# A one-layer mixer and mixture-of-experts step in float32: channel-major inputs for the prologue, and GpSimd in place of VectorE for the low halves of most weight units

## What is computed

```
h  = xn @ w_in                       # 1024 -> pool 512 | u 512 | v 512 | ca 512 | cg 512 | gates 3*1024
ya = pool_scale * (windowed mean of p, minus p) @ pool_w
yb = u * (tril(W_s) layer_norm(v) + b)                # chunks of 128 tokens
yc = silu(layer_norm(depthwise_conv31(ca * sigmoid(cg))))
merged = ga*(ya @ wb_pool) + gb*(yb @ wb_sgu) + gc*(yc @ wb_conv)
mixer  = merged @ w_out
moe    = top-1 of 4 groups, then top-2 of its 8 SwiGLU experts (1024 -> 512 -> 1024), 32 experts
```

## Time and profile before

| | us |
|---|---|
| median of three runs (1003.26 to 1004.27) | 1003.76 |
| the profiled execution | 1007.17 |
| its span, first to last instruction | 1005.4 |
| TensorE busy | 848.6 |
| VectorE busy | 353.4 |
| ScalarE busy | 201.4 |
| GpSimd busy | 65.8 |

### The profile page before, as it was taken

The page is one execution under the profiler, slowest core; times in us unless marked ns, Lnnn a source line. Parts: engine busy times, 40 slices in busy tenths (PEclk is TensorE's granted clock), DMA queues, the critical chain, the costliest instruction groups (busy, mean ns, idle before and its releaser), DMA issues.

```text
span 1005.4 us, 12484 instructions
## 1 busy us (share of the span) xinstructions
PE 848.6 (84%) x5203; PEld 581.2 (58%) x5203; DVE 353.4 (35%) x511; ACT 201.4 (20%) x300; POOL 65.8 (7%) x72
## 2 busy tenths in 40 slices
PE   3999999999999997997388898888878778877860
PEld 2999999999999997994133333333323232322320
DVE  3377686899577545204500000000000000000007
ACT  5321333222214323115001001100000000001003
POOL 0000000000000000000101111011101111011000
PEclk9999999999999998999599999999999999999995
DMA  9322221213315428544489999999999999999936
GB/s 296 94 85 85 84 85 54 79 49 105 106 50 181 168 63 312 196 169 163 163 323 419 419 419 419 417 418 417 421 417 419 420 419 419 419 419 419 417 151 252
DMA packets 73670, 262.16 MB, mean 261 GB/s; under 512 B 8999, under 2 KB 42947, under 8 KB 48480
## 3 DMA queue, kind: packets, MB, share of 16 engines
q1 hardware_dynamic: 68496, 252.44, 64.1%
q0 software_dynamic: 5120, 8.93, 2.4%
HBM read 256.08 MB, written 13.74 MB: 268 GB/s over the span
## 4 chain that ended last, share of the span: by engine, by line
PE 62%; DMA 19%; SPq 10%; DVE 5%; issue 2%; ACT 2%; POOLq 0%; DVEq 0%; ACTq 0%
PE ps L685 30%; DMA mem<-in_w_up_e 17%; PE ps L929 12%; SPq L550 10%; PE ps L720 9%; PE ps L950 5%; PE ps L653 1%; PE ps L917 1%; PE ps L814 1%; DMA mem<-expert_rows 1%; PE ps L940 1%; DVE xh L1669 1%; DVE xh L1676 1%; DVE mem L1635 1%; DVE xh L1668 0%
## 5 line engine op out<-in xcount | busy, mean ns | idle before, releaser
L929 PE MATMUL ps<-mem 128*64 128x512 f32 x1024 | 237.3, 618 | 28.0 <-DMA mem<-in_w_up_e 27.1
L929 PEld LDWEIGHTS ps<-mem 128*64 128x64 f32 x1024 | 81.9, 142 | 180.5 <-issue 179.3
L685 PE MATMUL ps<-x_high,w_high 128*128 128x272 f32 x640 | 173.8, 289 | 0.0
L1628 DVE TENSOR_TENSOR mem<-ps,ffn_cols 128x512 f32<-128x512 f32 x32 | 22.1, 692 | 431.1 <-PE ps L917 431.1
L685 PE MATMUL ps<-x_low,w_high 128*128 128x272 f32 x640 | 173.0, 289 | 0.0
L950 PE MATMUL ps<-mem 128*64 128x512 f32 x512 | 127.1, 642 | 14.8 <-ACT mem L1199 14.8
L685 PE MATMUL ps<-x_high,w_low 128*128 128x272 f32 x640 | 132.8, 289 | 0.0
L685 PEld LDWEIGHTS ps<-x_low,w_high 128*128 128x128 f32 x640 | 120.8, 189 | 0.1
L685 PEld LDWEIGHTS ps<-x_high,w_high 128*128 128x128 f32 x640 | 120.8, 189 | 0.1
L685 PEld LDWEIGHTS ps<-x_high,w_low 128*128 128x128 f32 x640 | 100.4, 189 | 0.0
L1266 DVE TENSOR_TENSOR w_low<-w_raw,w_high 128x2048 fp32r<-128x2048 f32 (+1 forms) x38 | 74.1, 1952 | 50.2 <-ACT w_high L1003 48.0
(11 more groups left out here) (224 smaller groups left out, 840.0 us busy)
## 6 DMA issues: line engine op xcount, KB each, us to landing
mem<-in_w_gate_e SPq DMA_DIRECT2D x32, 2048.0 KB, 34.0
mem<-in_w_up_e SPq DMA_DIRECT2D x32, 2048.0 KB, 33.8
mem<-in_w_down_e SPq DMA_DIRECT2D x32, 2048.0 KB, 34.1
w_raw<-in_w_in SPq DMA_DIRECT2D x22, 1024.0 KB, 5.1
w_raw<-in_w_out SPq DMA_DIRECT2D x4, 1024.0 KB, 6.7
mem<-expert_rows SPq DMA_DIRECT2D x4, 1024.0 KB, 9.6
xh<-in_x_prompt SPq DMA_DIRECT2D x4, 512.0 KB, 5.0
w_raw<-in_w_branch_pool SPq DMA_DIRECT2D x4, 512.0 KB, 3.5
```

The costliest lines, as they stand in the source:

```text
L685: last = pe.matmul(ps[:, 2 * r + half, 0:HT], w[:, k, c * P:(c + 1) * P], part[:, k, half * HT:(half + 1) * HT], start=(k == 0 and len(par ...
L929: last = pe.matmul(ps[g * CAP:(g + 1) * CAP, 2 + s].rearrange("p (m f) -> p m f", m=2), xgT[s][:, k % 4, (k // 4) * CAP:(k // 4 + 1) * CAP ...
L1628: v.tensor_tensor(xgT[s].rearrange("p c (h m) -> p c h m", h=2), ps[:, s].rearrange("p (c h m) -> p c h m", c=4, h=2), wide(ffn_cols[:].re ...
```

## The change

1. The host hands over x, the states, the vectors and the SGU weights with channels on partitions, and takes the new states back so. All transposes of the prologue, the two transposes of new states, the 32 tiny DMAs and 18 of the state stores go.
2. The sum of squares is taken over partitions: ACT and DVE square, DVE adds pairs, TensorE sums by a product with a column of ones, ACT takes the root, DVE inverts it and spreads it on a diagonal, TensorE broadcasts it (`ones` times `diag`) to PSUM, and DVE scales each x tile by it (`scale_x`).
3. Units 0 and 1 are split in halves of four k, and the first three column tiles are interleaved over k so that TensorE can start on tile k = 0.
4. GpSimd makes the low halves of units 2 to 37, in the order of the units, with the copies of states in its queue as well.
5. The branch for `AHEAD` in the expert loops is folded; the order of instructions stays as it was with `AHEAD = 0`.

```diff
@@ sync
-        for c in range(NCH):
-            src = d["x_prompt"][0][c * P:(c + 1) * P] if c < NCH - 1 else d["x_sample"].rearrange("b i n -> (b i) n")
-            sp.dma_start(x[0:chunk_rows(c), c], src).then_inc(x_loaded[c], 16)
-        sp.dma_start(cst[:], d["shape_constants"]).then_inc(const_loaded, 16)
...
+        sp.dma_start(cst[:, 0:CONST["before"].start], d["shape_constants"][:, 0:CONST["before"].start]).then_inc(ident_loaded, 16)
+        for i in range(KD // 2):
+            sp.dma_start(x_raw[:, 2 * i:2 * i + 2], d["x_channels"][:, 2 * i:2 * i + 2]).then_inc(x_loaded[i], 16)
+        sp.dma_start(param[:, 0:FG + KD], d["vectors"]).then_inc(param_loaded, 16)
...
+        for n in range(2):
             load_unit(n)
+        sp.dma_start(cst[:, CONST["before"].start:], d["shape_constants"][:, CONST["before"].start:]).then_inc(const_loaded, 16)
+        sp.dma_start(pool_before, d["pool_before"]).then_inc(states_loaded, 16)
+        sp.dma_start(conv_before, d["conv_before"]).then_inc(states_loaded, 16)
+        load_unit(2)
+        sp.dma_start(wsT, d["sgu_w_columns"]).then_inc(sgu_w_loaded, 16)
+        sp.dma_start(step_w, d["sgu_w_steps"]).then_inc(step_loaded, 16)
...
-                for b in range(NSEQ):
-                    r = slice(b * STEP, (b + 1) * STEP)
-                    sp.dma_start(out["pool_sample"][0][b, PH - STEP:PH], states[r, 1]).then_inc(states_stored, 16)
-                    sp.dma_start(out["conv_sample"][0][b, CH - STEP:CH], states[r, 3]).then_inc(states_stored, 16)
+                sp.wait_ge(states_out, 2)
+                sp.dma_start(out["pool_channels"], pool_after).then_inc(states_stored, 16)
+                sp.dma_start(out["conv_channels"], conv_after).then_inc(states_stored, 16)
@@ tensor
+        for i in range(KD // 2):
+            pe.wait_ge(pair_squared, i + 1)
             for c in range(NCH):
+                first = min(c * P, T - P)
+                last = pe.matmul(ps[:, 0, 0:NCH], squared_x[:, 2 * i, first:first + P], const["pick"][:, NCH - 1 - c:2 * NCH - 1 - c],
+                                 start=(i == 0 and c == 0), stop=(i == KD // 2 - 1 and c == NCH - 1))
+        pe.wait_ge(diag_ready, 1)
+        for c in range(NCH):
+            n = chunk_rows(c)
+            last = pe.matmul(ps[:, 6 + c // 4, (c % 4) * P:(c % 4) * P + n], const["ones"], diag[:, c, P - n:], start=True, stop=True)
...
+        for k in range(KD):
+            pe.wait_ge(act_took, act_has["xT", k])
+            for n, c, r in ((0, 0, 0), (0, 1, 1), (1, 0, 2)):
+                if k == 0 and c == 0:
+                    pe.wait_ge(first_low, n + 1)
+                if k == KD // 2 and c == 0:
+                    pe.wait_ge(low_ready, n + 1)
+                if r == 0:
+                    pe.wait_ge(dve_took, dve_has["xT", k])
+                last = tile_step(n, k, r, c)
...
-        state_rows(0, PH, lambda q: pext[:, q, SEQ:SEQ + PH], lambda q: pext[:, q, PH + SEQ:PH + T])
-        state_rows(4, CH, lambda q: cext[:, q, SEQ:SEQ + CH], lambda q: cext[:, q, CH + SEQ:CH + T])
@@ scalar
+        own(nc.scalar.activation(stat[:, 94:95], stat[:, 94:95], ACT.Sqrt))
+        for i in range(KD // 2):
+            act.wait_ge(x_loaded[i], 16)
+            nc.scalar.activation(squared_x[:, 2 * i], x_raw[:, 2 * i], ACT.Square).then_inc(x_squared, 1)
+        act.wait_ge(product, made["squares"])
+        nc.scalar.activation(stat[:, 5:5 + NCH], ps[:, 0, 0:NCH], ACT.Sqrt, scale=1.0 / D, bias=stat[:, 95:96]).then_inc(root, 1)
+        first_part(0, 0)
+        for k in range(4):
+            take_x(k)
+            if k < 3:
+                first_part((1, 0, 1)[k], (0, 1, 1)[k])
+        for k in range(4, KD):
+            take_x(k)
@@ vector
+        for i in range(KD // 2):
+            dve.wait_ge(x_loaded[i], 16)
+            own(v.tensor_tensor(squared_x[:, 2 * i + 1], x_raw[:, 2 * i + 1], x_raw[:, 2 * i + 1], ALU.mult))
+            dve.wait_ge(x_squared, i + 1)
+            v.tensor_tensor(squared_x[:, 2 * i], squared_x[:, 2 * i], squared_x[:, 2 * i + 1], ALU.add).then_inc(pair_squared, 1)
         dve.wait_ge(root, 1)
         own(v.reciprocal(stat[:, 10:10 + NCH], stat[:, 5:5 + NCH]))
+        v.tensor_tensor(diag, wide(ident.unsqueeze(1), [P, NCH, P]), wide(stat[:, 10:10 + NCH].unsqueeze(2), [P, NCH, P]), ALU.mult).then_inc(diag_ready, 1)
+        first_low_part(0, 0)
+        dve.wait_ge(product, made["spread"])
+        scale_x(0)
         for k in range(KD):
+            if k + 1 < KD:
+                scale_x(k + 1)
+            low_x(k)
+            if k < 3:
+                first_low_part((1, 0, 1)[k], (0, 1, 1)[k])
...
...
         glu(0)
-        low_part(3)
         glu(1)
...
         for j in range(NJ - 1):
             n = unit_no["branch", 0, j]
             merge(j, 0)
             merge(j, 1)
-            low_part(n + 2)
...
             for b in range(4):
...
-                if b in (0, 2):
-                    low_part(n + 4 + b // 2)
...
@@ gpsimd
+        pool.wait_ge(product, made["spread"])
         g.memset(pext[:, :, 0:PH], 0.0).then_inc(zeroed, 1)
+        pool.wait_ge(states_loaded, 32)
+        g.tensor_copy(pext[:, :, PH + T:]..., pool_before).then_inc(states_placed, 1)
+        g.tensor_copy(cext[:, :, CH + T:]..., conv_before).then_inc(states_placed, 1)
+        g.tensor_tensor(wsT, wsT, wide(const["causal"].unsqueeze(1), [P, KW, P]), ALU.mult).then_inc(sgu_masked, 1)
+        g.tensor_tensor(step_w, step_w, wide(const["blocks"][0:NS].unsqueeze(1), [NS, KW, NS]), ALU.mult).then_inc(steps_masked, 1)
+        def low_part(n):
+            s, kt = n % 3, depth(units[n])
+            pool.wait_ge(high_ready, n + 1)
+            g.tensor_tensor(w_low[s][:, 0:kt], w_raw[s][:, 0:kt], w_high[s][:, 0:kt].bitcast(F32), ALU.subtract).then_inc(low_ready, 1)
+        for n in range(2, 10):
+            low_part(n)
+        pool.wait_ge(p_extended, KW)
+        own(g.tensor_copy(pool_after[:, :, 0], pext[:, :, SEQ:SEQ + PH]))
...
+        for n in range(10, len(units)):
+            low_part(n)
```

More of the change, by code:

```diff
@@ L63 @@
 CONST, NCONST = _columns([
-    ("ident", P), ("causal", P), ("before", P), ("ones", P), ("blocks", NS),
+    ("ident", P), ("ones", P), ("pick", 2 * NCH - 1), ("before", P), ("causal", P), ("blocks", NS),
     ("expert", NE), ("group_of", NE), ("group", NG), ("place", P), ("block", NBLK), ("gather_row", 2 * NCH), ("scatter_row", 2 * NCH),
@@ L448, in program @@
     act_has = numbered(act_in_order)
[L450 removed]
+    dve_in_order = [("xT", k) for k in range(KD)] + tiles("ca") + tiles("pool") + ["sgu_steps"] + tiles("sgu")
     for j in range(NJ):
@@ L634, in _ @@
         sp.wait_ge(outs_stored, 16 * (1 + NCH))
-        sp.wait_ge(states_stored, 16 * (4 + 2 * NSEQ))
+        sp.wait_ge(states_stored, 16 * 2)
     @block.tensor
     def _(pe):
[L640 to L650, removed]
-            for c in range(NCH):
[L652 to L655, removed]
@@ L670, in _ @@
+        last.then_inc(product, 1)
+        pe.wait_ge(diag_ready, 1)
+        for c in range(NCH):
+            n = chunk_rows(c)
+            last = pe.matmul(ps[:, 6 + c // 4, (c % 4) * P:(c % 4) * P + n], const["ones"], diag[:, c, P - n:],
+                             start=True, stop=True)
         last.then_inc(product, 1)
@@ L691, in _, with tile_step @@
         xs = (x_high, x_low)
[L694 to L695 removed]
+        def tile_step(s, k, r, c):
             for half in range(2):
[L697 to L707 removed]
+                for w, part in ((w_high[s], x_high), (w_low[s], x_high), (w_high[s], x_low)):
+                    last = pe.matmul(ps[:, 2 * r + half, 0:HT], w[:, k, c * P:(c + 1) * P], part[:, k, half * HT:(half + 1) * HT],
+                                     start=(k == 0 and part is x_high and w is w_high[s]), stop=(k == KD - 1 and part is x_low))
+            return last
+        for k in range(KD):
[8 more added lines that the diff above has]
+                last = tile_step(n, k, r, c)
+                if k == KD - 1:
+                    last.then_inc(product, 1)
+        column_tiles(1, xs, KD, 3, 1).then_inc(product, 1)
+        s = weights_of("ca", 1)
+        for half in range(2):
+            pe.wait_ge(dve_took, dve_has["ca", half])
+            column_tiles(s, xs, KD, half, half).then_inc(product, 1)
+        s = weights_of("cg", 1)
+        for half in range(2):
+            pe.wait_ge(act_took, act_has["cg", half])
+            column_tiles(s, xs, KD, 2 + half, half).then_inc(product, 1)
         def token_chunks(lhs, s, half, free=None, tiles_ready=None):
@@ L1035, in _ @@
+        for k in range(4, KD):
+            take_x(k)
         act.wait_ge(const_loaded, 16)
-        nc.scalar.copy(before_ones[:].rearrange("p a n -> p (a n)"), cst[:, CONST["before"].start:CONST["ones"].stop]).then_inc(exact_ready, 1)
+        nc.scalar.copy(before_ones[:, 0], const["before"])
+        nc.scalar.copy(before_ones[:, 1], const["ones"]).then_inc(exact_ready, 1)
         high_part(2)
```

(10 more changed lines are left out.)

292 lines of the change are left out of this document (108 added, 184 removed).

## The result

The changed kernel takes 995.03 us (median of five runs, 993.36 to 997.14), the kernel before 1004.27 (five runs, 1003.26 to 1006.98): a ratio of 0.9907, 95% interval 0.9889 to 0.9925. Measured once more on another chip it is 995.29 against 1004.78, a ratio of 0.9899 (0.9884 to 0.9914). So it is faster by 9.2 us, where 20.2 were forecast (983.5): inside of the stated range of 976 to 996, with less than half of the forecast gain.

What follows compares the result with a forecast made beforehand. TensorE was taken to bound the mixer and DMA the experts' stretch; gains of 12.2 (prologue), 1.75 (transposes) and 7.5 (tail) less 1.2 (GpSimd) made 20.2 us, for 983.5 us, range 976 to 996.

Steps and rivals of the forecast that it cites:

- The prologue: Start of the kernel: TensorE's stream starts at 16.9 instead of 31.4 us; gain 12.2 us, bounds 8.5 to 14.2.
- five small float32 products with a weight load each: Prologue, after the last x: sums of squares on TensorE at 0.26 us per product, out of the array by 11.9 us.
- Transposes of states: Mixer: two sets of eight TensorE transposes go, with nothing hiding them; gain 1.75 us.
- GpSimd's subtraction: Mixer: low half of 2048 columns takes 5.0 us on GpSimd, over the cover at short units; loss 1.2 us.
- the bound from the memsets: GpSimd's subtraction: upper bound of 5.0 us, from memsets at 0.8 ns per column, three operands and a start of 0.1.
- The tail: Last merges before the output projection: shorter wait and no clock fall; gain 7.5 us, between about 2 and 9.5.
- TensorE can start there (six merged tiles are ready by 388.2): Tail: projection starts once unit 34's low half is ready at 391.3 us, then waits 0.3; gain 6.7 us.
- nearer to the upper end: Tail: 7.5 us taken between 2 and 9.5, as only four VectorE operations meet the two GpSimd subtractions.
- The lock: Rival: GpSimd subtractions and VectorE operations with two SBUF inputs exclude each other for their whole length; 993.4 us, chance 0.27.
- The slow start: Rival: VectorE paces the first interleaved tiles at 1.2 GHz; prologue gains 7 instead of 12.2, 988.5 us, chance 0.13.
- The experts' stretch took nothing back: Rival: the experts' weight stream, held by its own loads, gives the gain back; about 5 us stay, 999, chance 0.05.
- VectorE's 70 us off its load: Mixer: VectorE loses 36 subtractions, about 70 us; alone this brings nothing before 382 us, as TensorE doesn't wait for it.

Runs made afterwards that it cites:

- The one-pass version: Changed kernel with the sums of squares by one-pass fp32r products, squares rounded to fp32r before the channel sum: 991.01 us, ratio 0.9869.
- units 34 and 35 on VectorE: Changed kernel with the low halves of units 34 and 35, the first two of the projection, on VectorE instead of GpSimd: 991.33 us, ratio 0.9869.
- the last order of merges: Changed kernel with one-pass squares, all low halves on VectorE, last four merges reordered with PSUM reads ahead of the previous tile's low half: 984.84 us, ratio 0.9800.

## Why the forecast was wrong, by its own steps

*The prologue: 12.2 forecast, 7.0 found.* The step that failed is "five small float32 products with a weight load each, at the 0.26 us that a transpose took ... 11.9". A transpose is one record on TensorE, a float32 product two (0.43 us in all), and not five of them stood behind VectorE's last addition (10.9) but about eleven of the twenty: at 2.1 us for each pair of x tiles against 1.4 between the arrivals, TensorE had a queue from the first pair on. The root came at 15.5, 3.6 us late; the broadcast, five products of two records each, took 2.36 instead of 1.2. That is 4.7 of the 4.9 us by which the stream started late. The one-pass version, which halves the records of the sums alone, starts the stream 3.2 us earlier. The rest of the term was right: loads at 9.1 (the last square began at 9.4), 15.6 us of VectorE, and the stream itself took 20.97 where 18.3 + 1.4 + 1.0 = 20.7 stood, though in other shares (26 products in the first 5.9 us, a loss of 5.9 - 26 x 0.127 = 2.6 to the clock, and hardly any for GpSimd).

*Transposes of states: 1.75 forecast.* They are gone from the trace; no run takes them out alone, so their worth is taken over from the trace of before. The prologue and they together measured 7.6 by the medians.

*GpSimd's subtraction: 5.0 forecast, 4.60 found* where nothing is in its way. The 4.5 us of the Trainium skill (GPSIMD Engine Reference, Elementwise — side-by-side cycle accounting) was nearer than the bound from the memsets. TensorE lost about 1.6 us in the mixer where 1.2 stood, but by another path: little of it for the low half, which came in time at units 14, 18 and 22 and held up a weight load for 0.3 us at unit 30, and most of it at unit 18 for a merge that had been held up behind a TENSOR_SCALAR of 32 columns.

*The tail: 7.5 forecast, 2.6 found* (waits of 4.2 + 0.8 us for 7.2, and 0.4 of the clock). Two steps failed. First: "TensorE can start there (six merged tiles are ready by 388.2)". It can't: the projection's first wait is for VectorE's read of the last tile out of PSUM, which the forecast passed over; without any lock on the last four merges the wait is still 2.8 us (units 34 and 35 on VectorE). Second: "nearer to the upper end" between 9.5 and 2, on the ground that only four operations meet the two subtractions. One of them was enough, since it is in a chain: 4.33 us instead of 0.73, twice. The hole stayed long enough for the clock to fall (granted 0.86 from 388.0 to 405.7), and most of the 2.8 us of the clock stayed too: from 388.02 to 419.72 the first half takes 31.7 us, 0.8 of them the wait, against 28.45 for the second, which leaves 2.4.

*The rivals.* The lock was the right one: its 993.4 is 1.6 off the measured 995.0, with a prologue too good by 3 and a mixer too bad by 2, so the nearness of the sum is in part luck. It had 0.27, though the Trainium skill (SBUF — State Buffer, Who interferes with whom) states it plainly and the trace of before, with an idle GpSimd, couldn't speak against it. The slow start has the right 7 us for the prologue, for another reason: the clock did stay at 1.2 GHz for 5.9 us, but TensorE and not VectorE set the pace, and the start was late (its own sum is 988.7, not 988.5). The experts' stretch took nothing back: both kernels are at a DMA share of 1.01 there. VectorE's 70 us off its load were worth nothing by themselves, as forecast (986.68 with them on GpSimd, 984.84 without, once the tail is in order).

*What the goal of the change was worth.* The order of VectorE's last merges and low halves is worth more than the choice of the engine that makes the low halves: 6.8 us alone in the kernel before, against 1.5 for GpSimd.

## What to carry to other kernels

Before work is moved to GpSimd, mark the VectorE operations that share its way to SBUF and lie in a chain: each can be held up for the whole of GpSimd's instruction, and GpSimd for what is left of a gapless row of VectorE's. Where an engine waits ahead of a stage, list every semaphore of that wait (here a PSUM read as well as a low half) before a gain is booked for removing one. Price a float32 product by its records and its weight loads, and ask how many of them queue, not how many stand behind the last input.

## What the runs showed of the hardware

- The lock has two faces. VectorE second: 0.73 becomes 4.33 us, and 0.24 (the same instruction before and elsewhere) becomes 3.88 for a TENSOR_SCALAR with one SBUF tensor and 32 columns. The Trainium skill (SBUF — State Buffer, Who interferes with whom) lists tensor_scalar among the operations that can take both ports, so this agrees. GpSimd second: 13.54 us for 4.6 us of work, because it came in the middle of a row of taps without gaps and got in only at its end. Beside the first tap of a row (56.00) it got in behind that tap.
- Its grain is the single instruction: with 512 columns each, the hold-up of VectorE's merged low halves fell from 3.6 to at most 0.64 us.
- Forty float32 records with 5 columns each kept TensorE busy from 6.8 to 15.4 us, and the clock didn't rise in them: their weight loads took 333 ns to the last, as in the slow part of the stream (330), against 188 once the clock was up. The stream behind them ran its first 5.9 us at 1.2 GHz (26 products, 0.227 us each). With eleven products of 272 columns in the idle 2.6 us ahead of it, it was at 2.4 GHz from its third product on. Whether their kind did it or the closed gap, no run here separates.
- Before the projection, behind gapless work: after 2.8 us of waiting (units 34 and 35 on VectorE) the granted clock of the next 14.2 us is 0.88; with waits of 1.0 and 0.9 us (the last order of merges) it is 1.00 throughout.
